# Twelve projections of a gated recurrence: full-precision products replaced by three reduced-precision ones, with their weight halves and input split on two other engines

## What is computed

```
def hgrn2_mixer(h, w_in, lb, norm_g, w_out):
    proj = h @ w_in                                   # 256x1024 @ 1024x5120
    q, f_fw, f_bw, i_in, g = jnp.split(proj, 5, axis=-1)
    f = lb + (1.0 - lb) * sigmoid(f_logit)            # for f_fw and f_bw
    log f, 1 - f  per head                            # 8 heads of 128
    o = scan forward (q, 1 - f_fw, v, log f_fw) + scan backward (q, 1 - f_bw, v, log f_bw)
    o = rms_norm(o, norm_g) * silu(g)
    return o @ w_out
```

## Time and profile before

| | us |
|---|---|
| median of 3 runs | 3165.03 (3164.83 to 3166.06) |
| profiled execution, its own time | 3161.53 |
| its span in the trace | 3159.6 |
| PE busy | 3057.3 (97%) |
| DVE busy | 2252.5 (71%) |
| ACT busy | 1547.0 (49%) |
| stage of the twelve projections | from 1123.4 to 1207.0 of the span |

### The profile page before, as it was taken

How to read it: one execution, slowest core, us unless ns; L and a number is a source line. 1 busy time by engine, 2 the same in 40 slices (tenths; PEclk the granted TensorE clock), 3 DMA queues, 4 the chain that set the end, 5 groups by cost and what they waited for, 6 DMA issues and landing times.

```text
span 3159.6 us, 54295 instructions
## 1 busy us (share of the span) xinstructions
PE 3057.3 (97%) x19644; PEld 2764.3 (87%) x19644; DVE 2252.5 (71%) x3943; ACT 1547.0 (49%) x2638; POOL 369.4 (12%) x228
## 2 busy tenths in 40 slices
PE   8998999999999989899999999999999999999998
PEld 7986898898679978789999988887789999988887
DVE  7756896766575547679989965555578989975555
ACT  5535554554454433554544445554645444445554
POOL 5530563453010000000000000000100000000000
PEclk9999999999999999999999999999999999999999
DMA  8762676875235533045544455555435544445554
GB/s 324 281 251 81 243 290 222 296 278 213 80 107 186 186 133 120 28 161 182 184 147 140 140 173 193 193 193 201 145 121 180 182 158 140 140 166 193 193 193 152
DMA packets 124979, 567.89 MB, mean 180 GB/s; under 512 B 13872, under 2 KB 14000, under 8 KB 97328
## 3 DMA queue, kind: packets, MB, share of 16 engines
q1 hardware_dynamic: 108864, 504.41, 46.4%
q0 software_dynamic: 15264, 58.73, 4.9%
q10 hardware_dynamic: 720, 3.00, 0.2%
HBM read 565.03 MB, written 1.05 MB: 179 GB/s over the span
## 4 chain that ended last, share of the span: by engine, by line
PE 85%; DVE 5%; ACT 3%; issue 1%; POOL 0%; DMA 0%; DVEq 0%; ACTq 0%
PE turn L352 46%; PE gather L352 38%; ACT arena L1323 2%; DVE ring_low L2053 1%; PE turn L859 0%; DVE arena L2464 0%; DVE rounded L2064 0%; ACT L1323 0%; ACT hT L1323 0%; DVE arena L2323 0%; DVE arena L2185 0%; PE gather L653 0%; DVE arena L1963 0%; ACT rounded L1323 0%; DVE arena L2180 0%
## 5 line engine op out<-in xcount | busy, mean ns | idle before, releaser
L1323 ACT ACTIVATE dense<-ring 128x1024 fp32r<-128x1024 f32 x544 | 575.8, 1059 | 387.3 <-PE gather L352 346.1
L2486 DVE TENSOR_TENSOR ring_low<-ring,dense 128x1024 fp32r<-128x1024 f32 x544 | 662.3, 1218 | 78.1 <-ACT dense L1323 76.4
L352 PE MATMUL turn<-expert_src_high,dense 128*128 128x256 f32 x2304 | 665.5, 289 | 1.2 <-DVE expert_src_low L2045 1.2
L352 PE MATMUL turn<-expert_src_high,ring_low 128*128 128x256 f32 x2304 | 653.2, 283 | 0.0
L352 PE MATMUL turn<-expert_src_low,dense 128*128 128x256 f32 x2304 | 653.1, 283 | 0.0
L352 PE MATMUL gather<-dense 128*128 128x512 f32 x2048 | 631.6, 389 | 2.1 <-DVE ring_low L2486 2.1
L352 PE MATMUL turn<-rounded 128*128 128x256 f32 x2816 | 516.7, 286 | 20.8 <-DVE ring_low L2053 19.0
L2053 DVE TENSOR_TENSOR ring_low<-ring,rounded 128x1024 fp32r<-128x1024 f32 x264 | 416.7, 1596 | 164.5 <-ACT rounded L1323 164.2
L352 PEld LDWEIGHTS turn<-rounded 128*128 128x128 f32 x2816 | 447.1, 194 | 25.7 <-DVE ring_low L2053 20.9
L352 PEld LDWEIGHTS gather<-dense 128*128 128x128 f32 x2048 | 384.4, 188 | 82.8 <-DVE ring_low L2486 2.9
L352 PEld LDWEIGHTS turn<-expert_src_high,dense 128*128 128x128 f32 x2304 | 443.2, 192 | 1.8 <-issue 1.8
(11 more groups left out here) (240 smaller groups left out, 3841.3 us busy)
## 6 DMA issues: line engine op xcount, KB each, us to landing
ring<-tiles_in SPq DMA_DIRECT2D x544, 512.0 KB, 3.3
ring<-stream SPq DMA_DIRECT2D x205, 1024.0 KB, 5.0
arena<-ada_in POOLq DMA_DIRECT2D x96, 512.0 KB, 5.9
arena<-tables_in POOLq DMA_DIRECT2D x6, 1024.0 KB, 5.2
arena<-keys_in SPq DMA_DIRECT2D x2, 1024.0 KB, 7.7
arena<-c_in POOLq DMA_DIRECT2D x3, 512.0 KB, 5.8
hT<-x_in SPq DMA_DIRECT2D x1, 1024.0 KB, 5.0
x_rows<-rows_in ACTq DMA_DIRECT2D x1, 1024.0 KB, 17.2
```

The source lines that it names most:

```text
L352: return nc.tensor.matmul(out, lhsT, rhs, start=start, stop=stop, skip_group_check=True)
L1323: return nc.scalar.activation(out, in_, func, **kw)
L2486: V.tensor_tensor(tile_words(t, ring_low).bitcast(R32), tile_words(t), tile_high[:, t % AHEAD, :], ALU.subtract).then_inc(S("tile_low"), 1)
```

## The change

Pieces 0 to 11 of `hg_in` become split products. ACT copies each weight half (`hin_half`), DVE subtracts it (`hin_rest`), the input is split below (`source_high`, `source_low` into `hin_low`), and PE makes three fp32r products for each full one. Four buffers hold the high halves (`hin_high`), so the copy of half h waits until half h - 4 is used. Halves 0 and 1 are prepared between `ffn(3)` and the norm. In piece 0 both halves are worked chunk by chunk of the input. The 16 scans of a direction are issued as 8 and 8, with a subtraction behind each 8, and more subtractions stand between the other operations. The rest is bookkeeping: the counts of `source_ready` move from 4 + l to 5 + l.

```diff
+        hin_high = [hg_high[0], hg_high[1], over("hin_high2", hg_v_at, HALF), over("hin_high3", hg_v_at + HALF, HALF)]
+        hin_low = over("hin_low", LATE + KC * T, KC, T)
+        def hin_used(h):
+            i, b = divmod(h, 2)
+            return (S("half_used"), 4 * FFN_PIECES + i + 1) if b == 0 else (piece_done, piece_base("hg_in") + i + 1)
...
             def hgrn():
                 q0 = piece_base("hg_in")
-                for i in range(12):
-
-                    arrive(pe, q0 + i)
+                def product(i, b, k):
+
+                    h = 2 * i + b
+                    wh = hin_high[h % 4][:, k * P:(k + 1) * P].bitcast(R32)
+                    wl = ring_low[:, (q0 + i) % SLOTS, b * HALF + k * P:b * HALF + (k + 1) * P].bitcast(R32)
+                    xh, xl = expert_src_high[:, k, :].bitcast(R32), hin_low[:, k, :].bitcast(R32)
+                    out = B[i % 4][:, b * T:(b + 1) * T]
+                    mm(out, wh, xh, k == 0 and (i > 0 or b == 0), False)
+                    mm(out, wh, xl, False, False)
+                    return mm(out, wl, xh, False, k == KC - 1)
+
+                pe.wait_ge(S("low_ready"), part_base(4) + 2)
+                for k in range(KC):
+                    pe.wait_ge(S("source_ready"), KC * 4 + k + 1)
+                    for b in range(2):
+                        last = product(0, b, k)
...
+                for i in range(1, 12):
                     if i >= 4:
                         pe.wait_ge(S("hg_taken"), i - 3)
-                    project_pair(q0 + i, B[i % 4], hT, normed(6) if i == 0 else None).then_inc(piece_done, 1)
+                    for b in range(2):
+                        pe.wait_ge(S("low_ready"), part_base(4) + 2 * i + b + 1)
+                        for k in range(KC):
+                            last = product(i, b, k)
+                        done(last, b)
...
-                evacuate_end(6)
+                evacuate_end(6, source_high(6, expert_src_high))
...
+            def hin_half(h):
+
+                i, b = divmod(h, 2)
+                q = piece_base("hg_in") + i
+                if b == 0:
+                    arrive(act, q)
+                if h >= 4:
+                    act.wait_ge(*hin_used(h - 4))
+                run(hin_high[h % 4][:, :].bitcast(R32), ring[:, q % SLOTS, b * HALF:(b + 1) * HALF], ACT.Copy)\
+                    .then_inc(S("high_ready"), 1)
...
+                for h in (2, 3):
+                    hin_half(h)
                 for i in range(4):
-                    take(8 + i)
+                    hin_half(2 * i + 4)
+                    take(i)
+                    hin_half(2 * i + 5)
+                logs(0)
+                hin_half(12)
+                key_logs(0)
+                hin_half(13)
+                take(4)
+                for i in range(5, 8):
+                    hin_half(2 * i + 4)
+                    take(i)
+                    hin_half(2 * i + 5)
+                logs(1)
+                hin_half(20)
+                key_logs(1)
+                hin_half(21)
+                for i in (8, 9):
+                    take(i)
+                    hin_half(i + 14)
+                for i in (10, 11):
+                    take(i)
                 decays(0)
...
             ffn(3)
+            for h in range(2):
+                hin_half(h)
             layer_and_rms_norm()
...
-                rms_end(6)
+                rms_end(6, source_low(4, expert_src_high, hin_low))
...
+            def hin_rest(h):
+
+                i, b = divmod(h, 2)
+                s, cols = (piece_base("hg_in") + i) % SLOTS, slice(b * HALF, (b + 1) * HALF)
+                dve.wait_ge(S("high_ready"), part_base(4) + h + 1)
+                V.tensor_tensor(ring_low[:, s, cols].bitcast(R32), ring[:, s, cols], hin_high[h % 4][:, :],
+                                ALU.subtract).then_inc(S("low_ready"), 1)
...
             ffn(3)
+            for h in range(2):
+                hin_rest(h)
             layer_and_rms_norm(ends(3))
```

More of the change, by code:

```diff
@@ L1619, in decays, with logs @@
                                 .then_inc(S("hg_decays"), 1)
-                for d, (f, dst) in enumerate(((hg_bf, hg_eq[1]), (hg_bb, hg_ek[1]))):
-                    for i in range(4):
-                        take(4 * d + i)
+                def logs(d):
+                    f, dst = ((hg_bf, hg_eq[1]), (hg_bb, hg_ek[1]))[d]
                     act.wait_ge(S("hg_f_ready"), 8 * (d + 1))
@@ L2279, in halves, with forget @@
                     return buf.rearrange("p (h c) t -> p h c t", c=2)
-                for d, (f, kf) in enumerate(((hg_bf, hg_kf), (hg_bb, hg_kb))):
-                    for h in range(HG_HEADS):
-                        dve.wait_ge(S("hg_taken"), 4 * d + h // 2 + 1)
+                def forget(i):
+                    f = (hg_bf, hg_bb)[i // 4]
+                    dve.wait_ge(S("hg_taken"), i + 1)
+                    for h in (2 * (i % 4), 2 * (i % 4) + 1):
                         sl = slice(2 * h, 2 * h + 2)
@@ L2291, in hgrn, with scans @@
                     V.tensor_scalar(kf[:, :, :], kf[:, :, :], TINY, None, ALU.max).then_inc(S("hg_keys"), 1)
-                    logs = (hg_eq[1], hg_ek[1])[d]
+                def scans(d, k):
+                    f, logs = ((hg_bf, hg_eq[1]), (hg_bb, hg_ek[1]))[d]
                     t = slice(None, None, 1 if d == 0 else -1)
-                    for hc in range(2 * HG_HEADS):
-                        dve.wait_ge(S("hg_log"), 2 * d + hc // 8 + 1)
+                    dve.wait_ge(S("hg_log"), 2 * d + k + 1)
+                    for hc in range(8 * k, 8 * k + 8):
                         chain.add(V.tensor_tensor_scan(f[:, hc, t], ones, logs[:, hc, t], 0.0,
                                                        ALU.mult, ALU.add))
+                for h in (2, 3):
+                    hin_rest(h)
+                for i in range(4):
+                    hin_rest(2 * i + 4)
+                    forget(i)
+                    if i == 3:
+                        keys(0)
+                    hin_rest(2 * i + 5)
+                for k in range(2):
+                    scans(0, k)
+                    hin_rest(12 + k)
+                forget(4)
+                for i in range(5, 8):
+                    hin_rest(2 * i + 4)
+                    forget(i)
+                    if i == 7:
+                        keys(1)
+                    hin_rest(2 * i + 5)
+                for k in range(2):
+                    scans(1, k)
+                    hin_rest(20 + k)
                 dve.wait_ge(S("hg_key_logs"), 2)
                 chain.add(V.tensor_tensor(hg_kk[:, :, :], hg_kf[:, :, :], hg_kb[:, :, :], ALU.add))
+                hin_rest(22)
                 chain.wait()
                 chain.add(V.tensor_tensor(hg_kf[:, :, :], hg_bf[:, :, :], hg_eq[0][:, :, :], ALU.subtract))
+                hin_rest(23)
                 chain.add(V.tensor_tensor(hg_kb[:, :, :], hg_bb[:, :, :], hg_ek[0][:, :, :], ALU.subtract))
```

13 lines of the change are left out of this document (11 added, 2 removed).

## The result

| | before | after |
|---|---|---|
| median, us | 3164.93 (3164.14 to 3166.06, 4 runs) | 3148.83 (3146.65 to 3152.65, 4 runs) |
| profiled execution, us | 3161.53 | 3149.51 |
| its span, us | 3159.6 | 3147.6 |
| PE busy, us | 3057.3 | 3046.1 |
| DVE busy, us | 2252.5 | 2290.4 |

The ratio is 0.9947, with a 95% interval of 0.9934 to 0.9959: 16.1 us less where 11.0 were forecast. The time lies 5.2 us under the forecast and 2.5 us under the lower end of the range. Between the two profiled executions it is 12.0 us: 3149.51 where the prediction put 3150.5 on that scale.

What follows compares the result with a forecast made beforehand. PE was taken to bound the stage, with DVE becoming the bound before the first level. PE 12.7 us earlier, less DVE's 1.7, gave 11.0 us, passed to the end: 3165.03 - 11.0 = 3154.0, range 3151.3 to 3158.4.

Steps and rivals of the forecast that it cites:

- 6, behind the first level: After the first level's start, the engines depend on each other as before, so the 11.0 us pass to the end.
- 1. The products: PE, twelve pieces: a split piece takes 5.76 us instead of 6.91, so 13.8 us saved.
- 2. Halves 0 and 1: Their copies and subtractions behind ffn(3) cost nothing, with 0.1 us to spare; at most 1.2 us if the cover fails.
- 3. The start of piece 0: Input split before PE's first product: costs 0.9 us, so PE's last product is seen 12.7 us earlier, at 1194.5.
- 4. DVE's line: DVE behind piece 7: 30.0 us of work makes it the bound, 1.7 us later than PE's gain; level starts at 1204.5.
- Rival E: Clock rises early in piece 0, DVE's line starts 0.8 us earlier: 11.8 us less, 3153.2; chance 0.57 together with the forecast.
- 5. Hidden work: ACT's 22 copies and DVE's 22 subtractions inside the stage stay hidden: no PE wait, by 0.7 and 1.1 us.
- B: DVE subtractions cost 1.60 us instead of 1.16, lengthening its line 2.2 us: 8.8 us less, 3156.2; chance 0.11.
- D: DVE cannot feed PE through the stage: at 2.54 us a subtraction, 7.4 us slower, 3172.4; chance 0.04.
- The clock before the first level: PE idles 3.3 us there instead of 1.41; price 0 or 1.35 us, taken as 0.
- Rival A: PE's clock falls before the first level, costing 1.35 us: 9.7 us less, 3155.4; chance 0.18.
- Rival C: Gain is given back later, in the levels' chain over three engines: if half is lost, 5.5 us less, 3159.5; chance 0.10.

Runs made afterwards that it cites:

- gain held back: Changed kernel plus 36 full-precision products, result not used, on PE behind piece 12, before the first level: 3166.07 us, ratio 0.9992 to the kernel before.
- longer DVE line: Changed kernel plus two more 128x1024 subtractions, result not used, on DVE in front of the exponents: 3160.22 us, ratio 0.9976 to the kernel before.
- six pieces split: Changed kernel with only pieces 0 to 5 split and 6 to 11 full-precision again: 3153.98 us, ratio 0.9955 to the kernel before.

## Why the prediction was wrong in its size

The direction and the mechanism in the stage held. The step that failed is 6, behind the first level: it put nothing there beyond the 11.0 us passed on, and the executions show some 6 us more.

**1. The products.** Right, a little low. The takes of pieces 7 and 11 stand (1193.14 - 1170.32) / 4 = 5.71 us apart, where 5.76 were put in:

```profile
1170.32 0.60 ACT L1354 ACTIVATE arena<-turn 128x512 f32<-128x512 f32 x1 [1.71 <-PE turn L352]
...
1193.14 0.60 ACT L1354 ACTIVATE arena<-turn 128x512 f32<-128x512 f32 x1 [5.05 <-PE turn L352]
```

That is 0.119 us for a product. The 5.24 us a piece, the estimate that follows from the Trainium skill, "TensorE: Matmul & The Clock Gate", section "Back-to-back issue gap", is not reached here either.

**2. Halves 0 and 1.** Right. The statistics of bank 1 still wait for PE, by 0.25 us, and start at 1106.35, where they started at 1106.33:

```profile
1102.42 2.35 DVE L2122 TENSOR_TENSOR ring_low<-ring,hg_high 128x1024 fp32r<-128x1024 f32 x2
...
1106.35 0.69 DVE L1993 SCALAR_TENSOR_TENSOR arena<-x_rows,gather 128x512 f32<-128x512 f32 x1 [0.25 <-PE gather L352]
```

**3. The start of piece 0.** The first product is 1123.89 - 1121.10 = 2.79 us behind the scaled rows, as forecast. The excess of piece 0 was taken as 1.33; with the end of piece 7 at 1121.64 + 48.48 = 1170.12 (table of places), 1170.12 - 1123.89 - 8 x 5.71 = 0.6 was measured, near the 0.5 named for a clock that rises early. It did rise early: 1.00 from 1125 on. In other traces it rose later, and the piece took up to 0.6 us more in the changed kernel and up to 1.4 us more in its variants. The term was one value of something that varies from execution to execution.

**4. DVE's line.** Right: 1200.75 - 1170.95 = 29.8 us instead of 30.0, and 2.35 instead of 2.44 for `factors(0)`. That the line is the bound was shown by taking two operations out of it and by adding two. With the earlier end of piece 7 (1.2 us) the level starts at 1203.10 instead of 1204.5: 12.4 us of gain at this point, not 11.0. Rival E was that far right.

**5. Hidden work.** Right: PE never waited for `ring_low`, and in the line of step 4 a subtraction took 1.14 us from its start to the next (1188.12 to 1189.26), so rivals B and D did not come. A split piece takes no longer than 48 of its products.

**The clock before the first level.** Wrong. PE idled 3.1 us and the clock fell; the price was 1.63 us, where I took 0 over 1.35. Of the two rows in hand I went by the one nearest in idle time, 3.12 us. It was one value of two: in two of the four traces of before that very place paid 1.7 us. Rival A's mechanism happened in every trace of the changed kernel, and not with 1.41 or 0.49 us. The Trainium skill, "TensorE: Matmul & The Clock Gate", section "Why this matters for your kernels", warned of it; the traces agree at 3.1 and 5.6 us, and, in two of four each, at the 3.12 us of the earlier trace rows and the 2.75 us of the changed kernel at that place. E and A together leave 10.8 us, near the 11.0 of the forecast. That is luck: two errors cancel.

**6. Behind the first level.** This step failed, and with it the range's term for spread. I let 11.0 us pass to the end, and shifted both scales, that of the profiled execution and that of the median, by the same amount, with "about 1 us on either side for the spread of the runs shown". Those were three runs within 1.2 us of each other. (The ends of the range do not follow from it as they stand, either: with 1 us the lower end would be 3152.2, not 3151.3.) All 57 executions of the kernel before on record reach from 3156.4 to 3176.0, with a standard deviation of 3.4 us, and the profiled one of before (3161.53) lay 4.7 us under their mean of 3166.2. The mean of the 11 executions of the changed kernel is 3149.8. The difference is 16.5 us, with a 95% interval of 14.4 to 18.6, against 10.8 from the stage. So some 6 us come from elsewhere. The four traces a side show 3.5 of them, with a standard error of 2.7: 3.3 behind the stage and 0.2 ahead of it. Rival C looked for a change behind the first level too, but the other way.

**What stays open.** The stage's share is shown. The other 4 to 8 us are measured only as a difference of many executions. That most of them are the clock's is argued, not shown: the mean granted clock over the span is 0.9881 before and 0.9894 after (53 and 11 executions that have it on record), and 0.0013 of 3150 us is 4 us, as an estimate that takes PE to have had work all that time. In the traces 1.2 us are the load of one tile and not the clock. Why the lower clock should last shorter behind the change, at places whose code is the same, no run tells. That the gain held back still left some 3 us speaks against a cause that is only the earlier start of what follows. In all seven rows of the table with a changed kernel, the executions gain more than the stage does, by 1.3 us (longer DVE line) to 6.3 (six pieces split), and this surplus does not grow with the stage's gain.

## What to carry to other kernels

Where PE gets cheaper pieces, follow the engine that feeds its next dependent step, count everything that now stands in that line, and expect the bound to change sides there: here two of five subtractions in DVE's line cost at least as much as a split piece gained. An idle time of PE in front of a burst of matmuls can have a price in the clock, and one trace shows one draw of it: here the same place cost 0 or 1.7 us from execution to execution. So leave both prices in the range. Before a range is closed, ask how far executions of one program differ: three that agree within 1.2 us say little when the profiled one stands 3.5 us beside them.

## What was not expected of the hardware

- The same program has places at which a step of PE takes one of two or more durations, such as 21.6 or 23.2 us for 79 products and 13.1 or 14.4 us for 96. Those looked at stand behind an idle time of PE. The executions of the kernel before spread over 20 us in 3166; how much of that such places make was not added up.
- Products run through the idle time of the norm did not keep the clock. It was 0.88 over the transpositions and 0.50 right behind them, when the first split products ran.
- The idle time of 3.1 us in front of the level cost 1.63 us in all four traces of the changed kernel, and one of 5.6 us cost 2.65. One of 3.1 us elsewhere cost nothing in two of four traces and 1.7 us in the other two, and one of 2.75 us at that place did the same.
- The load of one tile took 4.0 to 4.7 us in the four traces of before and 3.2 to 3.5 in those of after, though its code is the same.
